# Expert passes of a mixture-of-experts trunk: the weight split of the piece two ahead is moved in front of the activation on ScalarE and in front of the product on VectorE

## The reference

```python
logits = (xt @ w_router) + b_router            # 256 tokens, 8 experts
top_logit, top_e = lax.top_k(logits, 2)
top_w = softmax(top_logit)
# for every expert e, over the tokens that chose it:
y = (silu(xb @ w_gate[e]) * (xb @ w_up[e])) @ w_down[e]      # 1024 -> 1408 -> 1024
x[token] += y * weight
```

## The kernel before

| j | 0, 1 | 2, 3 | 4, 5 | 6, 7 | 8, 9 | 10, 11 | 12, 13 | 14, 15 | 16, 17 |
|---|---|---|---|---|---|---|---|---|---|
| piece | gate 0 | up 0 | gate 1 | up 1 | down 0 | gate 2 | up 2 | down 1 | down 2 |

## Time and profile before

### The profile page before, as it was taken

How to read it: one execution, slowest core, us unless ns; L and a number is a source line. 1 busy time by engine, 2 the same in 40 slices (tenths; PEclk the granted TensorE clock), 3 DMA queues, 4 the chain that set the end, 5 groups by cost and what they waited for, 6 DMA issues and landing times.

```text
span 1085.0 us, 15652 instructions
## 1 busy us (share of the span) xinstructions
PE 1049.1 (97%) x5580; PEld 896.7 (83%) x5580; DVE 835.1 (77%) x1175; ACT 650.0 (60%) x905; POOL 28.5 (3%) x76
## 2 busy tenths in 40 slices
PE   6999999999999999999999989999999999999996
PEld 6888888889999997888888868778787878787885
DVE  3789897745445456689897676989998989898895
ACT  3757655444434345667655456776777677676773
POOL 6000000030000000000000000000000000000000
PEclk9999999999999999999999999999999999999999
DMA  9634555664464544634545484999899989898992
GB/s 260 211 123 156 176 161 186 226 197 166 164 214 155 193 158 156 193 129 156 175 158 192 137 290 165 318 323 354 285 353 319 349 287 375 304 340 293 357 323 94
DMA packets 125332, 248.74 MB, mean 229 GB/s; under 512 B 4912, under 2 KB 50034, under 8 KB 125280
## 3 DMA queue, kind: packets, MB, share of 16 engines
q1 hardware_dynamic: 123136, 243.02, 65.4%
q0 software_dynamic: 2144, 5.03, 1.9%
HBM read 246.99 MB, written 1.05 MB: 229 GB/s over the span
## 4 chain that ended last, share of the span: by engine, by line
PE 79%; DVE 11%; issue 4%; ACT 3%; DMA 2%; DVEq 0%; ACTq 0%; SPq 0%
PE bank L348 24%; PE bank L350 23%; PE bank L349 23%; DVE wlo L336 7%; ACT whi L329 2%; DMA ring<-in_w_in 2%; DVE h L1377 1%; PE bank L907 1%; PE bank L908 1%; DVE x L1375 1%; PE bank L927 1%; PE bank L967 1%; PE bank L928 1%; PE bank L616 0%; PE bank L606 0%
## 5 line engine op out<-in xcount | busy, mean ns | idle before, releaser
L336 DVE TENSOR_TENSOR wlo<-ring,whi 128x1024 fp32r<-128x1024 f32 (+2 forms) x506 | 540.9, 1122 | 96.6 <-ACT whi L329 96.0
L329 ACT CAST whi<-ring 128x1024 fp32r<-128x1024 f32 (+2 forms) x506 | 458.7, 973 | 33.5 <-PE bank L350 21.6
L348 PE MATMUL bank<-whi,hTh 128*128 128x512 f32 (+3 forms) x1152 | 409.7, 356 | 10.4 <-DVE wlo L336 8.6
L350 PE MATMUL bank<-whi,hTl 128*128 128x512 f32 (+3 forms) x1152 | 400.2, 347 | 0.0
L349 PE MATMUL bank<-wlo,hTh 128*128 128x512 f32 (+3 forms) x1152 | 400.0, 347 | 0.0
L348 PEld LDWEIGHTS bank<-whi,hTh 128*128 128x128 f32 x1152 | 218.8, 190 | 46.4 <-DVE wlo L336 17.5
L350 PEld LDWEIGHTS bank<-whi,hTl 128*128 128x128 f32 x1152 | 218.8, 190 | 23.3
L349 PEld LDWEIGHTS bank<-wlo,hTh 128*128 128x128 f32 x1152 | 219.1, 190 | 21.8 <-issue 0.5
L348 PE MATMUL bank<-whi,oTh 128*128 128x512 f32 x392 | 155.4, 397 | 3.8 <-DVE oTl L1825 2.4
L350 PE MATMUL bank<-whi,oTl 128*128 128x512 f32 x392 | 153.0, 390 | 0.0
L349 PE MATMUL bank<-wlo,oTh 128*128 128x512 f32 x392 | 153.0, 390 | 0.0
(11 more groups left out here) (299 smaller groups left out, 756.9 us busy)
## 6 DMA issues: line engine op xcount, KB each, us to landing
ring<-in_w_in SPq DMA_DIRECT2D x40, 1024.0 KB, 5.1
ring<-in_moe_w_down SPq DMA_DIRECT2D x40, 1024.0 KB, 5.9
ring<-in_moe_w_gate SPq DMA_DIRECT2D x32, 1024.0 KB, 7.0
ring<-in_moe_w_up SPq DMA_DIRECT2D x32, 1024.0 KB, 7.7
ring<-in_moe_w_gate SPq DMA_DIRECT2D x16, 768.0 KB, 6.1
ring<-in_moe_w_up SPq DMA_DIRECT2D x16, 768.0 KB, 4.5
ring<-in_ffn_w_gate SPq DMA_DIRECT2D x11, 1024.0 KB, 5.2
ring<-in_ffn_w_up SPq DMA_DIRECT2D x11, 1024.0 KB, 5.7
```

The lines of the kernel that those rows point to most:

```text
L329: nc.scalar.copy(whi[pc.part(hf)][:, 0:n], pc.raw[:, hf * n:(hf + 1) * n]).then_inc(hi_done, 1)
L336: nc.vector.tensor_tensor(wlo[q][:, 0:n], pc.raw[:, hf * n:(hf + 1) * n], whi[q][:, 0:n].bitcast(F32), ALU.subtract).then_inc(lo_done, 1)
L348: nc.tensor.matmul(o, sh, wh, start=start, stop=False)
L350: return nc.tensor.matmul(o, sl, wh, start=False, stop=stop)
```

## The change

In both loops over `ORDER` of the expert pass, the split of piece j + 2 is moved ahead of the operation on the finished product of piece j. On ACT `split_hi` of piece j + 2 stands ahead of the wait for piece j and the Silu (this matters for j = 1, 5, 11: pieces 3, 7, 13). On DVE `split_lo` of piece j + 2 stands ahead of the waits for piece j and the Silu, and of the product (j = 3, 7, 13: pieces 5, 9, 15). For other j the order of instructions is as before. No instruction, buffer or semaphore is added or removed, and nothing else in the program changes.

```diff
@@ ScalarE, expert_pass
                 for j, (kind, st, part) in enumerate(ORDER):
+                    if j + 2 < PASS_PIECES:
+                        split_hi(act_e, pc(j + 2), expert_half(j + 2))
                     if kind == "g" and part:
                         n = ESTEPS[st]
                         act_e.wait_ge(w_used, 2 * pc(j).number + 2)
                         nc.scalar.activation(esig[:, 0:n], bank[2][:, 0:n], ACT.Silu).then_inc(e_sig, 1)
-                    if j + 2 < PASS_PIECES:
-                        split_hi(act_e, pc(j + 2), expert_half(j + 2))
@@ VectorE, expert_pass
                 for j, (kind, st, part) in enumerate(ORDER):
                     n = ESTEPS[st]
+                    if j + 2 < PASS_PIECES:
+                        split_lo(dve, pc(j + 2), expert_half(j + 2))
                     if kind == "u" and part:
                         dve.wait_ge(w_used, 2 * pc(j).number + 2)
                         dve.wait_ge(e_sig, ES * p + st + 1)
                         V.tensor_tensor(eact[:, 0:n], esig[:, 0:n], bank[3][:, 0:n], ALU.mult).then_inc(e_act, 1)
-                    if j + 2 < PASS_PIECES:
-                        split_lo(dve, pc(j + 2), expert_half(j + 2))
```

## The result

The changed kernel takes 1067.25 us (median of 4, 1066.44 to 1068.76) against 1085.87 us before (median of 4 in the same comparison, 1084.7 to 1088.05). The ratio is 0.9828, 95% interval [0.9809, 0.9847]: 1.7% faster. The forecast direction and place were right, the range (1070 to 1079) was missed at its low end, by 2.75 us.

A forecast was written before the change was run, and what follows sets the result against it. PE, busy 97% of the span, was taken as the bound, so only its idle moments could be won. Gains at pieces 3, 7, 13, 16 and 11, less 0.45 for turn(0), made 14.0 us: 1086.11 - 14.0 = 1072.1; range 1070 to 1079.

The forecast's parts named there:

- piece 3, passes 1 to 7: PE's stall before piece 3 goes, its casts fitting in ACT's idle time: 7 x 0.43 = 3.0 us.
- piece 3 and turn(0), pass 0: In pass 0 a product 0.1 us later takes back all that piece 3 gives, so it counts nothing.
- piece 7: PE's stall before piece 7 goes in all 8 passes: 8 x 0.43 = 3.5 us.
- piece 16: PE's stall before piece 16, for the turned activations' low part, goes in passes 0, 2, 4, 6, 7: 3.7 us.
- piece 11: PE's stall before piece 11 goes in passes 0, 1, 3, 5: 1.13 + 3 x 0.44 = 2.4 us.
- turn(0), other passes: turn(0), waiting for DVE's later product, has no slack in passes 2, 4, 6: 3 x 0.15 = 0.45 us charged.
- just-in-time places: turn(0), turn(2) and piece 11 can fall late; 0.6 us at two places in 8 passes takes back 9 us: 1081.
- small gaps: Smaller gaps at other pieces of the passes could add up to 2 us of gain: 1070.
- (a): Rival: the product becomes PE's wait, turn(0) 0.6 us late in all 8 passes, costing 4.8 us: 1077; chance 0.21.
- (b): Rival: transfers set the pace at 49.7 us a pass, taking 3 of the 14 us back: 1075; chance 0.06.
- (c): Rival: no change, 1086, because the whi and wlo buffers are what is short; chance 0.06.
- (d): Rival: slower, 1098; DVE's move costs its full 2.27 us, early casts bring no lead, 11.4 us more; chance 0.07.

The follow-up runs named there:

- the repeat: The kernel before and the full change each run once more, unchanged: 1085.56 us and 1067.91 us.
- The repeat of before: The kernel before run once more, unchanged: 1085.56 us, ratio 1.0003.
- the repeat of after: The full change run once more, unchanged: 1067.91 us, ratio 0.9834 against the kernel before.
- VectorE's half: Against the kernel before, only DVE's splits move ahead of the product; ACT's casts stay behind the Silu: 1095.29 us, ratio 1.008.
- ScalarE's half alone: Against the kernel before, only ACT's casts move ahead of the Silu; DVE keeps the product ahead of the splits: 1072.72 us, ratio 0.987.

## Why the prediction was right, and where it was wrong

The steps, each as the difference between the traces of before and after at that place, summed over the passes (first two matmuls of a piece, as in the prediction):

| step | predicted us | measured us |
|---|---|---|
| piece 3, passes 1 to 7 | 3.0 | 3.1 |
| piece 3 and turn(0), pass 0 | 0 | 0.0 (+0.50 - 0.54) |
| piece 7 | 3.5 | 3.5 |
| piece 13, passes 2, 4, 6, 7 | 1.9 | 1.9 |
| piece 16 | 3.7 | 3.7 |
| piece 11 | 2.4 | 2.5 |
| turn(0), other passes | -0.45 | -0.1 |
| turn(2), pass 0 | 0 | -0.2 |
| piece 12, and piece 13 in passes 0, 1, 3, 5 | left out | 1.8 |
| all other matmuls | left out | 0.9 |
| sum | 14.0 | 17.0 |

**The mechanism was right at every step of the sum.** The just-in-time places held but for 0.04 us at turn(0) in passes 2, 4 and 6 and 0.2 us at turn(2) in pass 0, and in pass 0 the product takes back what piece 3 gives. There the product starts 11.87 us after the first matmul of piece 0 before and after alike, not 0.1 us later as the prediction has it. PE at turn(0) of pass 0, from the timelines of before and of after:

```profile
668.38 0.66 PE L967 MATMUL bank<-ident,act 128*128 128x128 f32 x4 [0.34 <-DVE act L1837]
...
665.89 0.55 PE L967 MATMUL bank<-ident,act 128*128 128x128 f32 x3 [0.89 <-DVE act L1839]
```

The prediction also called itself wrong if turn(0) waited 0.5 us or more. In pass 0 it waits 0.89 us. That sign did not fit the prediction's own working for pass 0, where a wait of 0.34 us was there already and the 0.50 us won at piece 3 had to come on top of it.

**What failed is a term of the sum**: the small gaps stood in it as nothing, and in the bound as "up to 2 us: 1070". They came to 2.7 us, and of the 0.45 us charged for turn(0) only 0.1 was due. The small gaps are of two kinds. Pieces 12 and 13 of the gather passes and of pass 0 had gaps of 0.3 us instead of 0.17, worth 1.8 us over 8 places. And a stall does not end with the second matmul: in the trace of before, starts after it come 0.23 to 0.24 us apart for a few matmuls instead of 0.227. All matmuls past the second of a group give 0.9 us. The stage gave 17.0 us instead of 14.0; with it the forecast would have been 1086.1 - 17.0 = 1069.1, already under the range. I put down the small gaps as a bound rather than as a term, though the trace of before has a start time for each. Nor did the range leave room at its low end for the spread of the time: the chances gave nothing to a time under 1070.

**The rest, 0.7 to 1.6 us, is not shown to be the change's.** The medians differ by 18.6 and, in the repeat, by 17.7 us, the stages by 17.0. The interval of the ratio stands for 16.6 to 20.7 us, so 17.0 lies within it. In both traces the part ahead of the stage is the same program, and it took 2.5 us less in the trace of after. Part of that is the granted clock. From the windows of before and after (columns as above):

```profile
228.00:236.00 8.00, 7.44 (x48) 7.21 (x49) 6.13 (x11) 7.14 (x10) 0.58 (x1) 0.79 0.44 158
```

```profile
228.00:236.00 8.00, 7.87 (x65) 7.87 (x66) 6.12 (x11) 6.76 (x10) 0.00 (x0) 1.00 0.55 197
```

Before, PE ran part of that window at 1.2 GHz instead of 2.4, after waits of 0.63, 0.67 and 0.55 us in the token norm, and was 1.5 us later behind it. The trace of after has the same three waits, 0.63, 0.67 and 0.55 us, and a granted clock of 1.00. The repeat of before shows 0.79 there again; the repeat of after and the six other kernels that are the same up to there show 1.00. Why it came in both traces of before stays open. The medians less the stages, 662.6 and 662.3 us against 661.0 and 661.7, leave it at most 1.6 us in the time. The remaining 1.1 us of the two traces stand within the first 32 us.

**The rivals.** (a), turn(0) late throughout, did not come: 0.54 us in pass 0 and 0.04 us in the passes 2, 4, 6. (b), transfers as the pace: the gather pass now moves 350 GB/s at a share of 0.97, and no wait of a cast for a transfer is listed in the stage. The pass without gather took 48.9 us, under the 49.7 that (b) allowed, and gave 2.2 us instead of 1.4. But it moved only 48.9 x 331 = 16.2 MB of the 17.3 that (b) counts for a pass, and the gather pass 18.4, so the ring evens the two out. Together they took 101.6 us, over the 99.4 of two passes at (b)'s rate. (b) falls by the missing waits; by its own rate, an estimate, little room is left above the transfers. (c), buffers: the stalls went with no buffer added, and with two pieces instead of three the stage of before grew by only 1.3 us, so it was order and not room that held the casts there; the Trainium skill's sentence on repeated gaps (page Perfetto Trace Analysis, section Optimization Strategy) says "can mean", and here the cause was the order of the instructions. But the same experiment shows its other side: without the third piece of buffers the better order gains nothing. (d) came only where VectorE's half stands alone.

## What to carry to other kernels

On an engine that works in order, whatever waits for the present result belongs behind the work for the next one that could already start; look for a row where the engine idles before an instruction while the buffers of the next are free. The same swap one engine further down pays only when the engine ahead has the lead: here 11.6 us lost without it, 3.4 us won with it. And when stalls are to be removed, sum every start-to-start gap over the regular distance, small ones and the slow matmuls behind them too; that sum, and not the big ones alone, is the forecast.

## What the runs showed of the hardware

- A wait costs PE more than the idle time shown. In the earlier trace rows the bracket says 0.17 us; the stall is 0.32 us by the first gap, 0.43 with the second, and removing it gave 0.44 and a few hundredths more in the following matmuls.
- The stage repeats to 0.05 us between executions of one kernel (423.29 and 423.27; 406.25 and 406.22) while the whole time spreads by 2 to 5 us; in the traces the start of the stage spreads by 6 us (652.1 to 658.3). Traces compared place by place told apart 0.76 us, which the 2 us of spread in the times hid.
- Stretches of 1.2 GHz came at different places in kernels that are the same up to there: the window 648 to 656, in which PE begins the gather after a wait of 2.3 us for pick_slots, has a granted clock of 0.79 with ScalarE's half alone and 1.00 with the full change. Four of the ten traces have it, and in these the stage starts 6.7 us after the first gather product, in the others 5.2.
